# Conditioning of a hybrid decoder layer: the first norm's columns first, the rest beside the input projections

## The reference, cut to what matters

```python
mod = silu(c) @ w_ada + b_ada                 # c: 9 rows; w_ada 1024 x 6144
sh1, sc1, gt1, sh2, sc2, gt2 = split(mod, 6)
h = rmsnorm(x, g_norm1) * (1 + sc1) + sh1
proj = h @ w_in                               # columns: u 512, z 1024, x|B|C 2048, dt 16, gates 2048
ya = s5_branch(u, ...)                        # complex diagonal scan, GLU
yb = mamba2_branch(z, causal_conv(xBC), dt, ...)
x = x + gt1 * ((gA * (ya @ w_branch_a) + gB * (yb @ w_branch_b)) @ w_out)
x = x + gt2 * peer(modulated rmsnorm of x)    # expert retrieval, gathers of rows
shf, scf = split(silu(c) @ w_ada_final + b_ada_final, 2)
```

## Time and profile before

| | us |
|---|---|
| three runs: lowest, median, highest | 2328.61, 2329.7, 2336.05 |
| the profiled execution: its time, its span | 2328.38, 2325.9 |
| stage_condition | 0 to 144.28 |
| stage_mix up to the first pass | 144.28 to 185.99 |
| the 16 passes | 185.99 to 391.05 |
| the rest of stage_mix | 391.05 to 429.30 |
| all later stages | 429.30 to 2325.9 |

### The profile page before, as it was taken

One profiled execution on the slowest core, in us unless ns is written; L12 is line 12 of the kernel. 1 busy time (PEld: TensorE's weight loads), 2 busy tenths in 40 slices (PEclk: granted clock), 3 DMA queues, 4 the chain that ended last, 5 costly groups with the idle time before them and its releaser, 6 DMA issues.

```text
span 2325.9 us, 20352 instructions
## 1 busy us (share of the span) xinstructions
PE 1319.9 (57%) x6420; PEld 760.4 (33%) x6420; DVE 1408.3 (61%) x3373; ACT 403.3 (17%) x869; POOL 1052.6 (45%) x1095
## 2 busy tenths in 40 slices
PE   4659999677667754567737657853224332323234
PEld 0237677563555433335414324520000000000000
DVE  3576777442676644486787677557665666665730
ACT  2101113501233321134220011211010110100100
POOL 0001112000335534355666565557656666766664
PEclk6679999788788877787769878875656665655557
DMA  9922222105679999899999999989989999999997
GB/s 342 332 76 99 106 86 91 75 1 210 246 283 373 371 368 339 307 349 327 353 394 378 399 402 399 365 336 388 354 327 364 365 359 356 379 359 368 348 353 274
DMA packets 249428, 697.74 MB, mean 300 GB/s; under 512 B 27003, under 2 KB 90139, under 8 KB 245183
## 3 DMA queue, kind: packets, MB, share of 16 engines
q0 software_dynamic: 149760, 545.33, 61.1%
q1 hardware_dynamic: 91838, 148.24, 18.1%
q10 hardware_dynamic: 7724, 2.89, 0.5%
HBM read 687.35 MB, written 9.15 MB: 299 GB/s over the span
## 4 chain that ended last, share of the span: by engine, by line
POOL 15%; DVE 14%; issue 13%; PE 9%; DMA 9%; another core or an unknown queue 8%; ACT 3%; SPq 2%; DVEq 2%; POOLq 0%; ACTq 0%
POOL arena L1757 7%; POOL arena L1777 7%; DVE arena L2464 7%; PE ps L2150 5%; DMA arena<-in_state_ssm_dram 4%; DMA arena<-in_expert_up_dram,rows 2%; PE ps L2118 2%; DMA arena<-in_expert_down_dram,expert 2%; SPq L1619 1%; DVEq L2405 1%; PE ps L1254 1%; DMA arena<-mod_scratch 1%; ACT arena L1823 1%; DVE arena L2412 1%
## 5 line engine op out<-in xcount | busy, mean ns | idle before, releaser
L2464 DVE CUSTOM_DVE_ANT_0 arena<-arena,ps 128x1024 f32<-128x1024 f32 x512 | 605.4, 1218 | 201.4 <-DMA arena<-in_expert_down_dram,expert 157.9
L2118 PE MATMUL ps<-arena 128*32 128x512 f32 x2048 | 376.0, 852 | 598.1 <-DMA arena<-in_expert_up_dram,rows 509.0
L1777 POOL DMA_INDIRECT arena<-in_expert_up_dram,rows x512 | 491.3, 960 | 388.2 <-remote 159.2
L1757 POOL DMA_INDIRECT arena<-in_expert_down_dram,expert x512 | 488.6, 954 | 322.8 <-issue 149.7
L2150 PE MATMUL ps<-arena 128*128 128x264 f32 (+1 forms) x1344 | 357.6, 425 | 114.7 <-ACT arena L1853 35.8
L2118 PEld LDWEIGHTS ps<-arena 128*32 128x32 f32 x2048 | 75.9, 137 | 837.2 <-issue 828.2
L2150 PEld LDWEIGHTS ps<-arena 128*128 128x128 f32 x1344 | 279.6, 212 | 196.7 <-issue 53.8
L789 PE MATMUL ps<-arena 128*128 128x256 f32 x640 | 142.4, 382 | 0.0
L789 PEld LDWEIGHTS ps<-arena 128*128 128x128 f32 x640 | 120.3, 190 | 27.5 <-issue 11.7
L678 POOL TENSOR_TENSOR arena<-arena 128x512 f32<-128x512 f32 x16 | 20.2, 1265 | 204.3 <-DVE arena L961 204.3
L1797 ACT ACTIVATE arena<-arena 128x8 f32<-128x8 f32 x65 | 13.5, 208 | 565.4 <-DVE arena L2464 297.4
(11 more groups left out here) (438 smaller groups left out, 1870.6 us busy)
## 6 DMA issues: line engine op xcount, KB each, us to landing
arena<-in_w_ada_dram SPq DMA_DIRECT2D x24, 1024.0 KB
arena<-in_w_in_dram SPq DMA_DIRECT2D x11, 2048.0 KB, 7.7
arena<-in_w_in_dram SPq DMA_DIRECT2D x20, 1024.0 KB
arena<-in_w_query_dram SPq DMA_DIRECT2D x16, 1024.0 KB
arena<-in_w_ada_final_dram SPq DMA_DIRECT2D x8, 1024.0 KB
arena<-in_w_out_dram SPq DMA_DIRECT2D x8, 1024.0 KB
arena<-in_expert_down_dram,expert POOLq DMA_INDIRECT x512
arena<-in_expert_up_dram,rows POOLq DMA_INDIRECT x512
```

What stands on the lines that cost most here:

```text
L1757: G.indirect_dma_start(U[i], None, down, bass.IndirectOffsetOnAxis(ap=at, axis=0))\
L1777: G.indirect_dma_start(Vr[r][j], None, up, bass.IndirectOffsetOnAxis(ap=at, axis=0))\
L2118: last = mm(ps[32 * j:32 * j + 32, c, :], Z[:, j, m, :], Vr[r][4 * half + j][:, c * 512:(c + 1) * 512], start=(p % 4 == 0 and m == 0), sto ...
L2464: V.tensor_tensor_reduce(U[i], U[i], row, 1.0, 0.0, ALU.mult, ALU.add, dots[n % 2][:, j:j + 1]).then_inc(s_uused, 1)
```

## The change

The two stages become one, `stage_front`, with no barrier between them.

- **Condition split.** x and the S5 parameters are loaded first, then the first eight 1 MB pieces of w_ada, each into a buffer of its own. The other 24 MB come in 48 pieces of 512 KB through a ring of two (`cring`), each piece being four matmuls of 256 columns, issued behind projection tiles by a list: of each six tiles of a group the tiles take 2, 1, 1, 2, 1 and 1 pieces. Bias: POOL (`add_bias`); copy out of PSUM: ACT (`crow`).
- **Modulation without the trip to DRAM.** DVE scales x by 1/rms only; PE turns it; the 2048 modulation values are turned by four transposes, and shift and scale are applied to the transposed activations, with one value per partition, by four operations on DVE and four on ACT.
- **S5 parameters transposed.** a_re, a_im and dt are turned first, and the arithmetic runs on 128 partitions by 16 columns (144 for the angles) in place of 16 by 128 (1152). B is loaded in rows of 8 KB and turned by 32 small transposes.
- **Projections.** The order of tiles is u, x, gA, z, gB. Weights come in 1 MB (256 columns) through a ring of three. Eleven tiles in place of four stand ahead of the passes; 33 in place of 40 within. The samples' 32 small products stand together ahead of the passes. The tables `RC` and `RS` are built on DVE beside the projections, with the softplus of dt behind them.
- **Convolution within the passes.** DVE runs one channel tile's three operations at the end of each pass, ACT its `silu` and the next `tap`. The output transposes move behind the GLU product.

```diff
-            for n in range(4):
-                load_w(n)
-            sp.dma_start(x[:, 0:NB, :], ...)
...
+            sp.dma_start(x[:, 0:NB, :], A["x_prompt"][0].rearrange("(b p) d -> p b d", p=P)).then_inc(s_x, 16)
...
+            for k in range(2, 8):
+                sp.dma_start(first8[k], wa[:, k, 0:2048]).then_inc(s_p[k], 16)
+            sp.dma_start(dtw, w_in_columns(A, C_DT, NH)).then_inc(s_dtw, 16)
...
+            for n in range(NP):
+                m = n // 2 + 3
+                if n % 2 and m < len(col0):
+                    sp.wait_ge(s_proj, n + 1)
+                    load_w(m)
+                for p in pieces_at.get(n, ()):
+                    if p + 2 < KD * BATCHES:
+                        sp.wait_ge(s_cpiece, p + 1)
+                        load_c(p + 2)
...
+    base = [4 + 40 * i // BATCHES for i in range(BATCHES)]
+    share = (2, 1, 1, 2, 1, 1)
...
+                for p in pieces_at.get(n, ()):
+                    i, k = p // KD, p % KD
+                    pe.wait_ge(s_cw[p % 2], 16 * (p // 2 + 1))
+                    if k == 0 and i:
+                        pe.wait_ge(s_crow, i)
+                    for j in range(4):
+                        last = mm(ps[strip(j, 32), 4, 256:512], cT[:, k, :], cring[p % 2][:, 256 * j:256 * j + 256], ...)
+                    last.then_inc(s_cpiece, 1)
...
+            for k in range(1, KD, 2):
+                h = mem.halves(Map.HTB + k * HW, HA, Map.OTHER)
+                S.activation(h, h, ACT.Identity, bias=mT[:, k, NS:NC_ROWS], scale=scT[:, k, NS:NC_ROWS]).then_inc(s_hS, 1)
...
+            def conv(n):
+                dve.wait_ge(s_tap, n + 1)
+                for j in (1, 2, 3):
+                    last = stt(out=ctmp[n % 4], in0=cv[:, n, j:j + HA], scalar=vT[...], in1=ctmp[n % 4],
+                               op0=ALU.mult, op1=ALU.add)
...
                 tt(q4, wi, c, ALU.mult).then_inc(s_part, 1)
+                conv(i)
```

More of the change, by code:

```diff
@@ L239, in stage_condition @@
[L239 to L251, removed]
@@ L271, in stage_condition @@
-    hparts = [(b, half) for b in range(5) for half in range(2)]
+    assert M <= work + 2 * KD * HW
+    hn = mem(F.u_at, CD, rows=3 * NS)
+    p3 = mem(F.ye_at, 3, P, rows=NS5)
+    M = F.gA_at
+    mod0 = take(512)
+    mT = take(16, NC_ROWS)
+    scT = take(KD, NC_ROWS)
+    gT = take(KD)
+    raw3 = take(3, NS5)
+    t = [take(NS5) for _ in range(8)]
+    wide = [take(NLEV * NS5) for _ in range(2)]
+    assert M <= F.ye_at
+    st_at = Map.KEEP
+    bias4, bias2 = mem(Map.YGB + 4 * HW, 4, 256), mem(st_at, 2, 256)
@@ new lines, in stage_front @@
+    cT = mem(st_at + 512, KD, 32)
+    bus = mem(st_at + NH * HD + L, 2 * P)
+    crow = [mem(st_at + 768, 256), mem(Map.HT + KD * HW + T, 256)]
+    sn_all, cs_all = (mem(F.pt_at + v * NS5, NLEV * NS5) for v in (V_SIN, V_COS))
+    trig = mem(F.pt_at + V_COS * NS5, 2 * NLEV * NS5)
+    so = mem(work + 2048, 2, P)
+    fo = mem(work + 2304, 2, P, rows=NS5)
+    wk = [mem(work + i * 512, 2, 256) for i in range(8)]
+    prod = [mem(Map.MG + Map.OTHER + i * 512, 2, 256) for i in range(4)]
+    part = [mem(Map.MG + i * 512, 2, 256) for i in range(4)]
@@ new lines, in stage_front @@
+    dtt = [mem(Map.GB + i * T, T, rows=NH) for i in range(6)]
+    ctmp = [mem(work + 1024 + i * HA, HA) for i in range(4)]
+    yg = mem(Map.HT + KD * HW + D, 4, HA)
+    dtk = mem(Map.HT + KD * HW, T, rows=NH)
+    ya = mem(tabs, 4, HA)
+    sg = mem(tabs + 4 * HA, HA)
+    ek = mem(tabs + 5 * HA, KD, P, rows=NH)
+    glu_w = mem(F.ring_at, 4, 512)
+    br_w = mem(F.ring_at + KD * 512, 4, D)
+    s_c, s_x, s_par, s_bias0, s_bn, s_vn, s_vec, s_st, s_hp, s_cn, s_dtw, s_bias = (
+        sem("in_" + n) for n in ("c", "x", "par", "bias0", "bn", "vn", "vec", "st", "hp", "cn", "dtw", "bias"))
@@ new lines, in stage_front @@
+    s_tap, s_conv, s_silu2, s_carry = (sem("sd_" + n) for n in ("tap", "conv", "silu", "carry"))
+    hparts = [(b, half) for b in range(5) for half in range(2)]
+    tiles = [("u", i) for i in range(4)] + [("x", i) for i in range(NCV)] + [("gA", i) for i in range(KD)] \
+        + [("z", i) for i in range(KD)] + [("gB", i) for i in range(KD)]
+    NP = len(tiles)
+    col0 = [C_U + 256 * i for i in range(2)] + [C_X + 256 * i for i in range(8)] + [C_G + 256 * i for i in range(4)] \
+        + [C_Z + 256 * i for i in range(4)] + [C_G + D + 256 * i for i in range(4)]
@@ L679, in _ @@
                 G.tensor_tensor(si, part[2], part[3], ALU.add).then_inc(s_S, 1)
+                while done < BATCHES and base[done] + 5 < loop_tiles(i)[0]:
+                    add_bias(done)
+                    done += 1
+            while done < BATCHES:
+                add_bias(done)
+                done += 1
             pool.wait_ge(s_sr, NS5)
@@ L733, in _ @@
                     evict(n)
+                if i >= 1:
+                    silu(i - 1)
+                if i + 1 < NCV:
+                    tap(i + 1)
                 if i in (6, 10, 14):
@@ new lines, in _ @@
+            last.then_inc(s_setps, 1)
+            first(range(2, 3))
+            pe.wait_ge(s_bn, 32)
+            for i in range(2):
+                rows = bnat[:, i, :].rearrange("s (q h) -> s q h", h=G5)
+                for h in range(G5):
+                    last = nc.tensor.transpose(ps[:, 2, (G5 * i + h) * NS5:(G5 * i + h + 1) * NS5], rows[:, :, h],
+                                               ident[0:NS5, 0:NS5])
+            last.then_inc(s_bnps, 1)
+            first(range(3, 5))
@@ new lines, in _ @@
+            for n, (b, half) in enumerate(hparts):
+                pe.wait_ge(s_xn, b + 1)
+                if n >= 2:
+                    pe.wait_ge(s_raw, n - 1)
+                m = rows_of(b)
+                for k in range(4):
+                    kk = 4 * half + k
+                    last = nc.tensor.transpose(ps[:, 3 + n % 2, k * P:k * P + m],
+                                               x[0:m, b, kk * P:(kk + 1) * P], ident[0:m, 0:m])
+                last.then_inc(s_hps, 1)
+            first(range(5, 8))
```

850 lines of the change are left out of this document (410 added, 440 removed).

## The result

The changed kernel took 2316.24 us in the median (11 runs), the kernel before beside it 2329.7: a ratio of 0.9932, 95% interval 0.9911 to 0.9954 (the two medians by themselves give 0.9942). That is faster by 0.7%. I had forecast 2286, a gain of 43.8; between the medians the gain was 13.5, and 2316 lies outside my range. The execution profiled took 2316.24, its span is 2314.5.

The account below looks back on a forecast made before the run. PE bounds the passes now; DVE would bound them after. Last y 39.0 us earlier (130 + 222 = 352 against 391.05) plus 4.8 behind it saves 43.8: 2328.4 - 43.8 + 1.3 = 2286 us, range 2260 to 2302.

Parts of the forecast that it names:

- the gaps here are short beside the work: In the passes: argument that new PE gaps of 1 to 3 us per pass would leave TensorE's clock at 1.00.
- the meeting: In each pass: DVE's three convolution operations wait for POOL's two over shared SBUF ports, 3.8 us in place of 1.4.
- this rival: In the passes: new gaps drop TensorE's clock to 0.50; all 16 passes slow would give 2466 us; chance 0.05.
- The late refills: 512 KB pieces queued behind 1 MB weight loads land 1.6 to 1.8 us late: 3 ahead of the passes, 13 within.
- DVE as the bound: In the passes: a DVE pass of 13.54 us exceeds PE's 12.4, so DVE sets the pace.
- the 222: Forecast length of the passes in us, from first `bu` to last y, along DVE's chain with fifteen passes at 203.1.
- The 13 us of late refills then lie mostly under it: In the passes: PE's waits for late pieces, 13 us, would mostly be hidden under DVE's 222 us chain.
- PE's work: In the passes: PE's own work at full clock, 174.0 plus 24.7 for the pieces, 198.7 us without late refills.
- The front: Everything ahead of the passes: dt starts at 45.0 and the first pass's `bu` at 130 in place of 185.99.
- my own upper bound, 43: In the front: end of the eighth piece if PE works off pieces 6 to 8 behind its 40 transposes; 39.7 taken.
- Samples' products with C: Ahead of the tiles: 32 small products 6.9 us, four semaphores 0.5, eight transposes of C 1.1.
- Behind the passes: From last y to the branch product: 16.3 us in place of 21.1, product still 15.7; saves 4.8.

Follow-up runs that it names:

- idle products: Changed kernel plus four extra full matmuls on PE ahead of each of ten late pieces' waits: ratio 0.9837 to the kernel before, passes 225.9 us.
- both edits: Changed kernel with 512 KB refills issued ahead of weight loads and the convolution ahead of DVE's wait for POOL: ratio 0.9688 to the kernel before, passes 200.3 us.
- the wide spread: Kernel with both edits, plus one pair of samples' small products behind each fourth step of tiles 3 to 10: ratio 0.9682 to the kernel before.
- one alone: Changed kernel with only the 512 KB refills issued ahead of the 1 MB weight loads: ratio 0.9808 to the kernel before, passes 219.5 us.
- the other alone: Changed kernel with only the convolution moved ahead of DVE's wait for POOL: ratio 0.9888 to the kernel before, passes 243.5 us.

## Why the prediction was wrong, step by step

**The step that failed** is in the rivals: "the gaps here are short beside the work", and the 0.05 that I gave the clock on it. I compared a gap of 0.75 between u tiles, behind which the clock had stayed, with gaps of up to 3 us between light work. Behind each of the seven waits of 1.6 us and more in the passes, `bu` and `y` ran slow, and so did five of the seven next tiles. My sum had this at nothing; PE's busy time in the passes was 226.05 against 199.47 for the same work at full clock, so it cost 26.6, more than the whole miss of 19.5 there. Keeping the clock, idle products paid for, gave 15.6 with the meeting and 20.7 without. My condition for this rival, that PE's own work per pass has to double before it shows, was also too coarse: no pass ran at 0.50 throughout, the clock stood at 0.89 over all of them.

**The late refills** were placed right and sized too small. All eight named in the passes came, the two ahead as well. In the changed kernel they made 15.5 of waiting in the passes where I had 13. With idle products in front, the six that could be measured were 3.1 late each against 1.6 to 1.8. With the pieces' loads first, too, a refill that I had landing 0.8 early was up to 0.76 late (with both edits 0.39). Whether my fixed part of a transfer or its rate was short, no run shows.

**DVE as the bound** held only as one of two. The meeting exists as forecast, 3.29 a pass against 3.8; a DVE pass took 12.85, not 13.54, and a chain worked out as mine was gives 211. No kernel shows the 222 as DVE's alone. With the pieces in time it was DVE that held the passes at 219.5, partly through the wait of `y` for L973, which my sum did not have; with late pieces PE held them and the meeting was worth nothing or 3. "The 13 us of late refills then lie mostly under it" failed with the clock and not by itself. With the clock kept, the late pieces and their idle products took the passes with the meeting from 219.5 to 225.9 only, and those without it from 200.3 to 222.8. At the low clock PE and its waits took 243.5 with no meeting at all, and nothing lay under DVE.

**PE's work** at full clock was right: 198.7 forecast without waits, 200.3 and 200.5 measured. A tile with its piece took 4.22 where I had 4.18.

**The front** was 13.1 late. dt 4.3: the eighth piece was there when I said (its product ends at 40.7 where PE asks early), but PE works off pieces 6 to 8 behind the transposes, from 41.13. Its last product there ends at 43.9. That is near my own upper bound, 43, and I had chosen the other end. dt, X and u: 43.0 for 42.8. Samples' products with C: 13.05 for 8.5, at a clock of 0.64, costed by me from pairs that stood between tiles at full clock; this is a second place where I put the clock at nothing, and the wide spread, which kept it, got 6.3 back. Tiles and pieces: 37.8 for 33.3, of which the first tile, still slow from the small products (5.70 for 3.72), has 2.0 and the two late pieces (4.6 for 3) 1.6.

**Behind the passes** 14.7 to the branch product for 16.3 forecast, and the product itself 14.1 for 15.7, so 3.2 better than I said. ScalarE's silus and taps cost nothing within the passes, as I had it: no wait of PE there is put down to ACT.

**A reading.** I wrote that PE was idle while DVE built the tables, 107.04 to 138.80. PE's last work there ends at 117.88, so it was idle from then on; no term of the sum uses this.

**The sum.** 13.1 (front) + 19.5 (passes) - 3.2 (behind them) and 0.5 for the close of the stage make 29.9 at its end, and 2.5 come in the stages behind, which is within their scatter. Their first 24.65 run at a clock of 0.58 where it was 0.72 before; what that costs I did not test. Together 32.4, which is the 43.8 forecast less the 11.4 between the spans.

## What to carry to other kernels

Where TensorE was the bound, each of seven waits of 1.6 to 3.3 us ahead of light work cost 1.7 to 4.8 us more in slow matmuls behind it (3.3 in the mean). So price each new wait twice, and price moved products by the clock of the place they move to, not of the place they leave. When two resources are near each other (here PE at 200 and DVE at 211), measure one fix with the other in place: one alone gave 22, the other alone nothing, both gave 41. Of two transfers on one queue, issue the one with the shorter lead first.

## What the chip showed unexpectedly

- The granted clock fell to 0.50 without any idle time: pairs of 32x8 products between the single 256-column steps of a tile were followed by it, while one pair behind every fourth step left it at 1.00.
- Putting 15.4 us of useless full matmuls into the passes, ahead of waits, made them 15.6 us shorter.
- POOL's operation pays for the meeting as well: 1.44 in place of 1.27.
